# Two transformer blocks in fp32: the residual stream with features on partitions instead of tokens

## What is computed

```python
# block 1, layer l (the same for ctx in layer 0, with its own shift, scale and gate)
hx = rms_norm(x, norm_mix_g[l]) * (1 + sc_a) + sh_a          # "mix"
x  = x + g_a * (mixer(hx) @ w_out[l])
h  = rms_norm(x, norm_ffn_g[l]) * (1 + sc_f) + sh_f           # "ffn"
g, u = split(h @ ffn_w_in[l], 2)
x  = x + g_f * ((silu(g) * u) @ ffn_w_out[l])
# block 2, layer i
h  = rmsnorm(x, norm1_g[i]); z = h @ w_in[i] + b_in[i]        # "n1"
qk = silu(causal_conv(z[..., :2048])); ...                    # "mqk": 4-tap convolution along tokens
rq, rk = rope(...)                                            # "rqk": rotation of pairs of features
x  = x + merged @ w_out[i]                                    # "w_out2"
h2 = rmsnorm(x, norm2_g[i])                                   # "n2"
x  = x + square(relu(h2 @ w_ff1[i] + b_ff1[i])) @ w_ff2[i] + b_ff2[i]
h3 = rmsnorm(x, norm3_g[i])                                   # "n3"
x  = x + sigmoid(h3 @ w_pe_gate[i]) * (p[i] @ w_pe[i])        # "pe_g", "w_pe"
# after both: rmsnorm(x, final_g)
# rmsnorm(x, g) = x * rsqrt(mean(x*x over the 1024 features) + 1e-6) * g
```

## Time and profile before

| | us |
|---|---|
| median of 3 runs | 2721.96 |
| fastest, slowest run | 2718.68, 2724.55 |
| the profiled execution's own time | 2721.37 |
| span in its trace | 2719.6 |

### The profile page before, as it was taken

The page is one execution under the profiler, slowest core; times in us unless marked ns, Lnnn a source line. Parts: engine busy times, 40 slices in busy tenths (PEclk is TensorE's granted clock), DMA queues, the critical chain, the costliest instruction groups (busy, mean ns, idle before and its releaser), DMA issues.

```text
span 2719.6 us, 32844 instructions
## 1 busy us (share of the span) xinstructions
PE 2461.0 (90%) x14092; PEld 2066.7 (76%) x14092; DVE 1217.6 (45%) x1554; ACT 998.6 (37%) x1214; POOL 1427.2 (52%) x316
## 2 busy tenths in 40 slices
PE   4977979999998989899889987999988998988997
PEld 3764669788897766897778775788868977768895
DVE  2767542221236465311566336253549444443462
ACT  3235532212223133433453332443446433334343
POOL 1321023233445500677576675678846766566884
PEclk8988989999999989899999999999989999989998
DMA  6440024444323140355455343345535534334552
GB/s 257 155 179 8 25 100 157 154 155 170 140 96 119 65 93 17 140 186 186 159 175 189 140 174 128 140 156 186 194 113 189 192 142 172 138 139 150 186 193 94
DMA packets 61672, 390.76 MB, mean 144 GB/s; under 512 B 6616, under 2 KB 11096, under 8 KB 16344
## 3 DMA queue, kind: packets, MB, share of 16 engines
q1 hardware_dynamic: 61528, 388.67, 39.4%
HBM read 387.60 MB, written 1.05 MB: 143 GB/s over the span
## 4 chain that ended last, share of the span: by engine, by line
PE 73%; DVE 16%; ACT 4%; DMA 3%; issue 2%; POOL 2%; SPq 0%; DVEq 0%; ACTq 0%
PE PS L458 21%; PE PS L459 20%; PE PS L460 20%; PE PS L572 2%; POOL w_lo L971 2%; PE PS L603 2%; PE PS L527 2%; PE PS L645 1%; DMA raw<-chunks_in 1%; PE PS L789 1%; DVE SCR L1746 1%; DVE SCR L1745 1%; PE PS L585 1%; DVE free_b L1688 1%; ACT w_hi L994 1%
## 5 line engine op out<-in xcount | busy, mean ns | idle before, releaser
L971 POOL TENSOR_TENSOR w_lo<-raw,w_hi 128x2048 fp32r<-128x2048 f32 x300 | 1415.0, 4730 | 1169.3 <-ACT w_hi L994 1169.3
L994 ACT ACTIVATE w_hi<-raw 128x2048 fp32r<-128x2048 f32 x300 | 571.1, 1913 | 729.6 <-PE PS L460 460.0
L458 PE MATMUL PS<-x_hi,w_hi 128*128 128x256 f32 x2080 | 594.8, 286 | 7.2 <-POOL w_lo L971 5.4
L459 PE MATMUL PS<-x_lo,w_hi 128*128 128x256 f32 x2080 | 591.4, 284 | 0.0
L460 PE MATMUL PS<-x_hi,w_lo 128*128 128x256 f32 x2080 | 591.2, 284 | 0.0
L458 PE MATMUL PS<-w_hi,x_hi 128*128 128x512 f32 (+1 forms) x992 | 398.9, 402 | 37.5 <-POOL w_lo L971 30.5
L458 PEld LDWEIGHTS PS<-x_hi,w_hi 128*128 128x128 f32 x2080 | 402.4, 193 | 22.5 <-issue 13.4
L459 PEld LDWEIGHTS PS<-x_lo,w_hi 128*128 128x128 f32 x2080 | 402.5, 194 | 0.2
L460 PEld LDWEIGHTS PS<-x_hi,w_lo 128*128 128x128 f32 x2080 | 402.1, 193 | 0.0
L459 PE MATMUL PS<-w_lo,x_hi 128*128 128x512 f32 (+1 forms) x992 | 393.1, 396 | 0.0
L460 PE MATMUL PS<-w_hi,x_lo 128*128 128x512 f32 (+1 forms) x992 | 392.2, 395 | 0.0
(11 more groups left out here) (257 smaller groups left out, 2545.9 us busy)
## 6 DMA issues: line engine op xcount, KB each, us to landing
raw<-chunks_in SPq DMA_DIRECT2D x348, 1024.0 KB, 4.8
bias_ring<-brows_in SPq DMA_DIRECT2D x36, 256.0 KB, 5.0
free_b<-rel_in SPq DMA_DIRECT2D x4, 512.0 KB, 7.7
BIG<-rel_in SPq DMA_DIRECT2D x4, 512.0 KB, 8.4
G<-nrows_in SPq DMA_DIRECT2D x1, 2048.0 KB, 8.7
tabt<-tabs_in SPq DMA_DIRECT2D x1, 1632.0 KB, 12.5
G<-nrows_in SPq DMA_DIRECT2D x1, 1536.0 KB, 6.6
X<-x_in SPq DMA_DIRECT2D x1, 1024.0 KB, 8.5
```

What stands on the lines that cost most here:

```text
L458: pe.matmul(o, lhs[0], rhs[0], start=start, stop=False, **more)
L459: pe.matmul(o, lhs[0], rhs[1], start=False, stop=False, **more)
L971: pool.tensor_tensor(w_lo[:, c % RING, :], ring[:, c % RING, :], w_hi[:, i % HI_RING, :].bitcast(F32), ALU.subtract).then_inc(*lo_ready.no ...
L994: act.activation(w_hi[:, i % HI_RING, :], ring[:, n % RING, :], ACT.Copy).then_inc(*hi_ready.now(n))
```

## The change

X is stored with features on partitions: `X[p, who, k, t]`, feature 128k + p, `who` for x or ctx. All that follows from it:

- The norm's sum runs over partitions. ACT squares X slab by slab (128 features; L1047 of the changed file), DVE adds the slabs up (L1420), PE multiplies with ones (`sum_of_squares`, L545), ACT takes the root (`deviation`, L1072), DVE the reciprocal of 128 x 512 or 128 x 256 (`inverse_root`, L1428). There are no transposes of xn.
- mix and ffn norms: DVE scales each slab (L1438), ACT applies scale and shift (L1093) and makes the high part (L1087), DVE the low part (L1443).
- n1, n2, n3: X times the gain is written as high and low part slab by slab as the residual is finished (`tails` on ACT, `finish` on DVE, L1460), and the product starts on it. 1/rms is applied when the result leaves PSUM: by a DVE step `scale` ahead of ACT's bias in mqk, rqk and ff1, in `biased` by a per-token scalar, in pe_g by DVE ahead of the sigmoid. The ones product stands behind the first chunk of mqk or ff1.
- Gates are per-partition scalars in the residual's one DVE step (L1614). POOL's diagonals, the ones products and the copies to G are gone.
- w_out, ffn_out, w_out2, ff2, pe_g and w_pe are made in `project_feat`; ffn_in(0) and ffn_out(0) are 512 wide, with one bank for each slab. w_pe stands before pe_g. The first unit of mqk stands before the gate product. Relu moves to DVE (`max`, then `mult`). The modulation chunks stand in twos behind two weight chunks from w_out(0) on. PE waits for the late tables after swiglu(1).
- The inputs x and ctx and the output are laid out in the new order on the host; the output leaves in two DMAs.

```diff
-        X = place("X", 4 * D)[0][:, :].rearrange("p (t d) -> p t d", t=4)
+        X_ = place("X", 4 * D)[0]
+        X = X_[:, :].rearrange("p (w k t) -> p w k t", w=2, k=KD)
...
-        def gate_list(l):
-
-            return [(kind, who, half) for kind in (2, 5) for who in range(2 - l) for half in range(2)]
-
-        def gate(l, kind, who):
-            n = gate_list(l).index((kind, who, 0))
-            return G[:, n * 512:n * 512 + 1024]
+        def gate(l, kind, k, who):
+
+            return modc[l][:, kind * 8 + k, who:who + 1]
 
...
+            def project_feat(st, l, n, rhs, freed, width=256, k_tiles=KD, n0=0, need=None, between=None):
+
+                per = 512 // width
                 for j in range(n0, n0 + n):
-                    for kg in range(2):
+                    for kg in range(-(-k_tiles // KC)):
                         if need and j == n0:
                             pe.wait_ge(*need(kg))
                         c, w = take_chunk(st, l)
-                        for g in range(groups):
-                            pair = (j * groups + g) % 2
-                            if kg == 0:
-                                claim(2 * pair, 2 * pair + 1)
-                            for s in range(4):
-                                for kt in range(KC * kg, KC * kg + KC):
-                                    mm = product(PS[:, 2 * pair + s // 2, (s % 2) * 256:(s % 2) * 256 + 256],
-                                                 [a[:, kt - KC * kg, s * P:(s + 1) * P] for a in w],
-                                                 [a[:, kt, g * 256:g * 256 + 256] for a in rhs],
-                                                 kt == 0 and s % 2 == 0, kt == KD - 1, True)
-                            if kg == 1:
-                                ends(mm, c, st, l, j, g)
-                                reader[2 * pair] = reader[2 * pair + 1] = freed.after(st, l, j, g)
-                            elif g == groups - 1:
-                                mm.then_inc(*projected.now(("chunk", c)))
+                        last = kg == (k_tiles - 1) // KC
+                        for s in range(4):
...
+            def sum_of_squares(key, tiles, columns=False):
+
+                acc, n, b = sums[tiles][0], tiles * P, 7
+                pe.wait_ge(*x_summed.after(key, KD - 1))
+                claim(b)
+                mm = pe.matmul(PS[:, b, 0:n], tab("ones"), acc, start=True, stop=True)
+                if columns:
+                    for t in range(2):
+                        mm = pe.matmul(PS[:, b, n + t:n + t + 1], acc[:, t * P:(t + 1) * P], tab("ones")[:, 0:1],
+                                       start=True, stop=True)
+                mm.then_inc(*sums_bc.now(key))
+                reader[b] = std_ready.after(key)
+
...
-                ev_in(0, norm(("mix", 0), 4))
+                ev_in(0, copied(("mix", 0)))
...
-            pe.wait_ge(*tab_in.after())
...
-            need = norm(("mix", 1), 4)
-            project_tok("od_q", 1, 2, KD, tokens(hT[4]), 1, need=need)
+            sum_of_squares(("mix", 1), 4)
+            project_tok("od_q", 1, 2, KD, tokens(hT[4]), 1, need=copied(("mix", 1)))
...
+            pe.wait_ge(*tab_in.after())
...
-                pe.wait_ge(*norm(("n1", l), 2)(1))
+                project_feat("mqk", l, 1, hT[2], freed=evicted("mqk", l), need=copied(("n1", l)), between=after_first(("n1", l)))
...
+                sum_of_squares(("n3", l), 2)
+                project_feat("pe_g", l, 2, hT_b, need=copied(("n3", l)),
+                             freed=lambda j, i: scaled.after("pe_g", l, 2 * j + i))
+            sum_of_squares("out", 2)
...
-            def diagonals(l):
-
-                pool.wait_ge(*(mod_stored.after(0, 1) if l == 0 else x_ready.after("ffn_out", 0)))
-                for n, (kind, who, half) in enumerate(gate_list(l)):
-                    if (l, n) == (0, 0):
-                        pool.wait_ge(*turned.after("kn", 3))
-                    if (l, n) == (0, 4):
-                        pool.wait_ge(*attended.after("mla", 15))
-                    k = kind * 8 + 4 * half
-                    columns = modc[l][:, k:k + 4, who:who + 1].to_broadcast([P, 4, P])
-                    pool.tensor_tensor(G[:, n * 512:(n + 1) * 512].rearrange("p (k d) -> p k d", k=4),
-                                       ident.unsqueeze(1).to_broadcast([P, 4, P]), columns,
-                                       ALU.mult).then_inc(*gate_diag.now(l, n))
-
...
+            def tail(key, k, write=True):
+
+                if write:
+                    act.activation(hT_of(key)[0][:, k, :], X[:, 0, k, :], ACT.Copy,
+                                   scale=gain_of(key, k)).then_inc(*copied_s.now(key, k))
+                square(key, 2, k)
...
+            def deviation(key, tiles, columns=False):
+
+                n = tiles * P
+                act.wait_ge(*sums_bc.after(key))
+                if columns:
+                    act.activation(stat[:, 8:10], PS[:, 7, n:n + 2], ACT.Sqrt, bias=eps, scale=1.0 / D)
+                act.activation(sums[tiles][1], PS[:, 7, 0:n], ACT.Sqrt, bias=eps,
+                               scale=1.0 / D).then_inc(*std_ready.now(key))
...
+                    act.wait_ge(*scaled.after(key, k))
+                    for w in range(tiles // 2):
+                        o = full[tiles][:, k, w * 256:w * 256 + 256]
+                        ins = act.activation(o, o, ACT.Identity, bias=modc[l][:, kind * 8 + k, w:w + 1],
+                                             scale=modc[l][:, kind * 8 + 8 + k, w:w + 1])
...
+                    act.wait_ge(*scaled.after("mqk", l, j))
...
+                        at = 1024 * (j % 2) + 256 * s
+                        ins = act.activation(conv_in[:, s, 3:259], SCR[:, at:at + 256], ACT.Identity,
...
-            def gated_add(st, l, j, g, pair, gate_of, xs):
-
-                tmp = SCR[:, 1024:2048].rearrange("p (t n) -> p t n", t=2)
-                dve.tensor_tensor(tmp[:, 0], PS[:, 2 * pair, :], gate_of[0], ALU.mult).then_inc(*vec_chain.now())
-                dve.tensor_tensor(tmp[:, 1], PS[:, 2 * pair + 1, :], gate_of[1],
-                                  ALU.mult).then_inc(*stored.now(st, l, j, g))
-                dve.wait_ge(vec_chain.sem, vec_chain.count)
-                dve.tensor_tensor(xs[:, 0], xs[:, 0], tmp[:, 0], ALU.add).then_inc(*x_ready.now(st, l, j, g, 0))
-                dve.wait_ge(stored.sem, stored.count)
-                link(dve.tensor_tensor(xs[:, 1], xs[:, 1], tmp[:, 1], ALU.add), x_ready, st, l, j, g, 1)
-                x_ready.alias(st, l)
-
...
+                        for k in ks:
+                            for w in range(whos):
+                                at = 256 * w if l == 0 else 256 * (k % 2)
+                                ins = dve.scalar_tensor_tensor(X[:, w, k, :], PS[:, bank, at:at + 256], gate(l, kind, k, w),
+                                                               X[:, w, k, :], ALU.mult, ALU.add)
...
+            def finish(key, ks, write=True):
+
+                for k in ks:
+                    if write:
+                        dve.wait_ge(*copied_s.after(key, k))
+                        hi, lo = (a[:, k, :] for a in hT_of(key))
+                        dve.scalar_tensor_tensor(lo, X[:, 0, k, :], gain_of(key, k), hi.bitcast(F32), ALU.mult,
+                                                 ALU.subtract).then_inc(*copied_v.now(key, k))
+                    add_square(key, 2, k)
...
+            def inverse_root(key, tiles, columns=False):
+
+                r = sums[tiles][1]
+                dve.wait_ge(*std_ready.after(key))
+                if columns:
+                    dve.reciprocal(stat[:, 8:10], stat[:, 8:10])
+                link(dve.reciprocal(r, r))
...
+                        ins = dve.scalar_tensor_tensor(o[:, t, :], PS[:, 2 * (j % 2) + t, :], rstd_col[t],
+                                                       bias_ring[:, b % 2, :], ALU.mult, ALU.add)
...
+                def scale(st, j, bank, o):
+
+                    dve.wait_ge(*projected.after(st, l, j, 1))
+                    dve.tensor_tensor(o, PS[:, bank:bank + 2, :].rearrange("p b (s t) -> p (b s) t", s=2),
+                                      bc(rstd, [P, 4, 256]), ALU.mult).then_inc(*scaled.now(st, l, j))
...
+                    scale("rqk", j, 2 * (j % 2), SCR[:, 0:1024].rearrange("p (s t) -> p s t", s=4))
...
-                    link(dve.tensor_tensor(s, s, s, ALU.mult))
+                    link(dve.scalar_tensor_tensor(s, s, 0.0, s, ALU.max, ALU.mult))
```

More of the change, by code:

```diff
@@ L59 @@
 MOD_BANKS = 3
-EARLY_TABS = 130
+EARLY_TABS = 258
 RING = 4
@@ L1295, in _ @@
                 copy_turned(("mg", l))
-                norm(("n2", l), 2, "w_out2", l)
+                tails(("n2", l), "w_out2", l)
                 for j in range(8):
@@ L1314, in _ @@
-            norm("out", 2, "w_pe", 1)
+                tails(("n3", l), "ff2", l)
+                for b in range(4):
```

(6 more changed lines are left out.)

699 lines of the change are left out of this document (388 added, 311 removed).

## The result

The changed kernel takes 2730.41 us as a median of five runs (2729.09 to 2735.14), against 2721.96: ratio 1.0037, 95% interval 1.0023 to 1.0052, so it is slower by 0.37%. A second measurement (`after_again`) gave 2731.57 and 1.0038. The forecast was 2720, with 0.40 on faster and 0.38 on slower: the time lies in the range, the sign went to the smaller side.

The account below looks back on a forecast made before the run. The prediction took PE's stream plus its holes as the bound (PE busy 2461.0 of 2719.6 us). Its terms summed to -1.0 against 2721.4, giving 2720, with a range of 2690 to 2746.

Parts of the forecast that it names:

- term 10: ff1: scale in front, relu moved to DVE; DVE 10.8 us a unit against PE 11.5; 0, at most +4 a layer.
- rival B: ff1 turns DVE-bound once DVE's steps pass 8.2 us a unit; +26, 2746 us; chance 0.14.
- term 8: Convolution stage of block 2, the largest term: scale, bias and tap in series, POOL locks stay; +18.7 a layer, +37.4.
- Its ring: Convolution stage: DVE's scale, ACT's bias and tap, then DVE's locked steps in series, 18.6 us a unit instead of 13.6.
- Rival A: Convolution loops cost only the scale's own time, ACT's bias and tap staying beside DVE's steps; 2694 us; chance 0.27.
- term 5: n1: product starts early, scaled at eviction; hole -7.0 in layer 0, -6.3 in layer 1; stall from 1285.9 loses 2.5.
- block 1: From the first product on: dense products, gates, norms that still stop PE, and the stall before n1; -18.2 us.
- The gates: 24 ones products of 512 and their waits for ACT's copies go; -11.4 us.
- Term 1: Dense products in new widths, 512-wide ones with the weight moving priced at 0.233 us; sum -3.5 us.
- the start: No xn transposes and a late wait for the tables: first product at 45 to 49 instead of 58.73; -12 us.
- Rivals C: The start gives nothing, first weights or late slabs hold PE, dense products at 0.2275; 2737 us; chance 0.07.
- D: At n1 to n3 PE still waits for all slabs and the inverse root, halving the -39; 2740 us; chance 0.06.

Follow-up runs that it names:

- e_all_pt: Changed kernel with convolution accumulator, rotation and ff1 in PSUM, plus the split of p moved from behind ff1's unit 5 to behind unit 7: 2643.72 us, ratio 0.9717.
- e_before_psum: Kernel before the change, with convolution accumulator, one rotation operand and ff1's Relu and square in PSUM, nothing else changed: 2691.75 us, ratio 0.9890.

## Why the prediction was wrong

**Wrong: term 10, ff1, "0, at most +4 a layer".** The stage grew by 12.5 where the form of ff2 (45.96 instead of 44.57, twice) and the ones products explain 3.4: 9.1 a layer, 18.3 in all, more than the whole miss of 8.6. The two waits make 5.0 of it, and the pace behind them some 3:

```profile
1823.40:1835.00 11.60, 11.60 (x85) 11.60 (x86) 0.88 (x1) 1.92 (x1) 11.60 (x3) 0.86 0.40 159
...
1908.50:1920.00 11.50, 11.48 (x83) 11.50 (x84) 9.69 (x4) 5.44 (x6) 11.21 (x3) 0.85 0.36 134
```

85 products at 0.120 would take 10.2. The granted clock is 0.86 there: PE was partly at 1.2 GHz behind a wait of 2 us. Two things went wrong in the step. It compared sums (10.8 of DVE in 11.5 of PE) where the order mattered: the lock falls on the steps just ahead of the scale, and scale, bias, copies and POOL follow in series, so a late scale reaches PE even though DVE has spare time. The sums even moved the other way: DVE's three steps took 158.4 us in before, where PE had no wait in the stage, and 142.7 in after. The series of 3.3 that belonged beside them stood only in rival B, whose own limit of 8.2 us a unit was passed (142.7 over 16 units is 8.9). And it did not list everything that the change moved: the split of p went from a place without POOL to one with it, 417 ns to 4836, and `e_all_pt` shows that with ff1's own locks gone it alone makes the second wait. Rival B had the mechanism and the sign but the wrong price (+26 with one wait per unit; there is one per half).

**Undersized: term 8.** Its ring was right to 0.1 (18.6 a unit forecast, 18.7 measured), its stage came to +22.2 and +20.8 instead of 19.3 with the ones products. Of the 22.2 in layer 0, 13.0 are longer waits of PE (21.7 instead of 8.6), 0.7 the ones products, and the other 8.5 PE's pace behind the holes, which the term put at nothing: 96 products took 12.97 and 13.22 us behind the waits of 3.24 and 7.58, and 11.40 where none stood. Its split into "locks" and "scale, bias, tap" as things that add up did not hold either: alone they cost 7.8 and 6.0, together 30.0. Rival A ("only the scale's own time", `mo` near 94) fell with the locks in place; without them `mo` came at 83.3.

**Too hopeful: term 5 in layer 1**, -3.0 instead of -6.3: the hole is 10.5, not 7.2. Together these miss by 26 on the slow side.

**More than forecast on the other side: block 1**, -28.6 instead of -18.2, which hid part of that. This is in part luck of the execution: from the first product to the hole at n1 after took 1224.0, the other changed kernels with the same block 1 up to 1230.8, and the kernel before 1252.7, but 1247.9 in `e_before_psum`, whose block 1 is that of the kernel before. So the gain lies between 17 and 29. w_out(0) took 3.8 us less, ffn0's hole shrank by 2.7 instead of growing by 0.6, ffn(1) lost 4.4 instead of 0.7, mix1 grew by 4.9 instead of 7.4, and ffn_in(0) and ffn_out(0) gave 19.7. The gates were the exception: those of layer 1 had covered a wait for DVE, which PE now has in the open (10.4 instead of 7.8 ahead of the attention). rv to w_out2 and the holes at n2 and n3 gave another 6 more than forecast. Term 1's 0.233 came out (192 products of ff2 in before took 44.57), but not its reason, the weight as moving operand: the weight moves in `mo` too, at 0.2275.

**Right:** the start (46.28, in 45 to 49, by the luck of an unlocked step: five of the eleven executions lie above 49), n1 of layer 0, the holes at n2 and n3 to 15%, the rotation stage, pe_g with w_pe, the end, and the reciprocals:

```profile
L1428 DVE RECIPROCAL G<-G 128x256 f32<-128x256 f32 x8 | 14.0, 1747 | 22.1 <-ACT G L1072 22.1
...
L1428 DVE RECIPROCAL G<-G 128x512 f32<-128x512 f32 x3 | 10.1, 3352 | 13.3 <-ACT G L1072 13.3
```

Rivals C and D fell: the first product came early, and n1's hole was 4.9.
